# Merge stage of a hybrid decoder step: who says that a weight buffer is free, who copies the high parts, and how the sample sums reach the branch outputs

## The reference, cut to what matters

```
for each branch n:   m += sigmoid(x @ w_gate[n] + b_gate[n]) * (o_n @ w_branch[n])
x  = LN(ALPHA * x + m @ w_out);   x = LN(ALPHA * x + MoE(x))
```

## Time and profile before

| what | us |
|---|---|
| median of 3 runs (lowest, highest) | 1377.12 (1375.39, 1379.11) |
| the profiled execution's own time | 1373.24 |
| its span, first to last instruction | 1371.4 |
| TensorE busy (matmuls) | 1286.0, 94% of the span |
| VectorE busy | 944.2, 69% |
| ScalarE busy | 609.6, 44% |
| merge stage, 393.82 to 873.73 | 479.91 |

### The profile page before, as it was taken

How to read it: one execution, slowest core, us unless ns; L and a number is a source line. 1 busy time by engine, 2 the same in 40 slices (tenths; PEclk the granted TensorE clock), 3 DMA queues, 4 the chain that set the end, 5 groups by cost and what they waited for, 6 DMA issues and landing times.

```text
span 1371.4 us, 19929 instructions
## 1 busy us (share of the span) xinstructions
PE 1286.0 (94%) x7596; PEld 1087.6 (79%) x7596; DVE 944.2 (69%) x1492; ACT 609.6 (44%) x910; POOL 224.9 (16%) x199
## 2 busy tenths in 40 slices
PE   9999999998999999999999999999989999999970
PEld 5788657785589999999999999787748778888850
DVE  3674454433558878887877543466779799999957
ACT  4453565323642113121212112221338788898867
POOL 0200000007022322211010000000356212211130
PEclk9999999999999999999999999999989999999995
DMA  8223301002046776345553432322599986778986
GB/s 248 62 80 116 133 1 37 25 1 93 1 155 216 248 256 230 130 150 198 186 177 135 166 119 89 124 75 80 189 359 352 369 273 232 271 267 284 408 225 247
DMA packets 75011, 240.22 MB, mean 175 GB/s; under 512 B 16661, under 2 KB 27140, under 8 KB 61086
## 3 DMA queue, kind: packets, MB, share of 16 engines
q1 hardware_dynamic: 48630, 160.80, 32.5%
q0 software_dynamic: 17584, 61.31, 14.4%
q10 hardware_dynamic: 8704, 16.84, 3.4%
HBM read 215.65 MB, written 65.76 MB: 205 GB/s over the span
## 4 chain that ended last, share of the span: by engine, by line
PE 75%; DVE 6%; ACT 5%; DMA 4%; issue 2%; POOL 0%; SPq 0%; DVEq 0%; POOLq 0%; ACTq 0%
PE ps L568 18%; PE ps L570 17%; PE ps L569 17%; PE ps L1662 5%; PE ps L1693 3%; PE ps L1694 3%; PE ps L1695 3%; PE ps L1825 3%; PE ps L1865 2%; DMA b<-in_w 2%; DMA b<-in_w_merge 1%; ACT b L999 1%; ACT b L995 1%; ACT b L911 1%; PE ps L1857 1%
## 5 line engine op out<-in xcount | busy, mean ns | idle before, releaser
L568 PE MATMUL ps<-b,b 128*128 128x344 f32 (+2 forms) x1488 | 525.1, 353 | 9.0 <-DVE b L1016 5.0
L570 PE MATMUL ps<-b,b 128*128 128x344 f32 (+2 forms) x1488 | 516.3, 347 | 0.0
L569 PE MATMUL ps<-b,b 128*128 128x344 f32 (+2 forms) x1488 | 516.0, 347 | 0.0
L568 PEld LDWEIGHTS ps<-b,b 128*128 128x128 f32 (+1 forms) x1488 | 279.9, 188 | 33.6 <-DVE b L1016 5.6
L570 PEld LDWEIGHTS ps<-b,b 128*128 128x128 f32 (+1 forms) x1488 | 279.6, 188 | 24.5
L569 PEld LDWEIGHTS ps<-b,b 128*128 128x128 f32 (+1 forms) x1488 | 279.9, 188 | 21.1
L839 ACT ACTIVATE b<-ps,b 128x344 f32<-128x344 f32 x96 | 52.5, 548 | 276.6 <-PE ps L570 276.4
L1431 DVE TENSOR_TENSOR b<-b,b 128x2048 fp32r<-128x2048 f32 x64 | 146.5, 2291 | 19.4 <-ACT b L911 18.0
L1662 PE MATMUL ps<-b,b 128*128 128x128 f32 (+1 forms) x786 | 115.1, 278 | 14.3 <-DMA b<-tmp_xs 3.1
L911 ACT CAST b<-b 128x2048 fp32r<-128x2048 f32 x64 | 123.4, 1929 | 11.3 <-DMA b<-in_w 7.2
L1662 PEld LDWEIGHTS ps<-b,b 128*128 128x128 f32 (+1 forms) x786 | 91.1, 143 | 40.8 <-DMA b<-tmp_xs 5.2
(11 more groups left out here) (306 smaller groups left out, 1607.7 us busy)
## 6 DMA issues: line engine op xcount, KB each, us to landing
b<-in_w SPq DMA_DIRECT2D x96, 1024.0 KB
b<-in_w_merge SPq DMA_DIRECT2D x32, 640.5 KB, 4.0
tmp_xs<-b ACTq DMA_DIRECT2D x32, 514.0 KB, 4.1
b<-tmp_xs SPq DMA_DIRECT2D x32, 514.0 KB
b<-in_w_in SPq DMA_DIRECT2D x6, 1024.0 KB, 7.6
b<-in_xT SPq DMA_DIRECT2D x4, 1024.0 KB, 11.9
b<-in_w_out SPq DMA_DIRECT2D x4, 1024.0 KB, 8.5
b<-in_x SPq DMA_DIRECT2D x8, 512.0 KB, 4.1
```

Source lines behind the costliest of these rows:

```text
L568: mm(out, hi, mhi, start=start, stop=False)
L569: mm(out, hi, mlo, start=False, stop=False)
L570: return mm(out, lo, mhi, start=False, stop=stop)
```

## The change

Three edits are made together.

1. The loads of merge weights wait for the users of the buffer, not for `merge_free`. The first two are loaded as before. Weight j then waits for `mb` and `sgd` to have reached 3j-3: TensorE's last branch matmuls of unit 3j-4, and ScalarE's sigmoid of that unit (which reads the bias in the buffer). VectorE's increment of `merge_free` at each weight's end goes.
2. The six high parts of the branch outputs are copied by ScalarE, behind the sigmoid (and the weight copy) of units 4, 7, 35, 36, 41 and 44. VectorE's low parts move to units 8, 11, 38, 41, 45 and 48, and wait for the copy.
3. The partition sums of four samples are taken at once. `heads_out` goes. `partition_sums` has the ones as the stationary operand, 32 columns wide, and the sample's 256 values as the moving one; four samples go to four groups of 32 output partitions. It runs after units 37 and 41 for C and 57 and 72 for A. ScalarE copies the 512 columns of the bank out (at units 41 and 72), TensorE transposes them (four transposes, after units 42 and 73), and `decode_out` adds them at units 42 and 73 (before: 41 and 72), now by two adds. There are four pairs of accumulators instead of two, and VectorE waits for them in fewer places. SyncE's load of `w_out` waits for the transposes after unit 73 instead of for the sums after unit 72.

```diff
@@ emit_sp2
-                        w0 = sp.snap(i * 2 + (1 + u), min_val=1, max_val=4 * KD)
+                        used = sp.snap(i * 6 + (3 * u - 3), min_val=3, max_val=12 * KD)
-                        sp.wait_ge(S("merge_free"), w0)
+                        sp.wait_ge(S("mb"), used)
+                        sp.wait_ge(S("sgd"), used)
-            merge_weights(0, 26)
+            sp.wait_ge(S("merge_free"), 2)
+            for u in range(2):
+                sp.dma_start(wg[:, u, :], a["w_merge"][u]).then_inc(S(f"wg{u}"), 16)
+            merge_weights(2, 26)
             sp.wait_ge(S("mb"), 72)
-            sp.wait_ge(S("heads"), N("heads", 2 * NB))
+            sp.wait_ge(S("sums_T"), N("sums_T", 2))
@@ emit_pe2
+            def partition_sums(br, r):
+                pe.wait_ge(S("dv"), 4 * r + 4 if br else NB + 8 * r + 8)
...
+                for g in range(4):
+                    m = mm(ps[32 * g:32 * g + 32, 7, r * W:(r + 1) * W], one[:, 0:1].to_broadcast([P, 32]), acc_of(br, 4 * r + g),
+                           start=True, stop=True)
                 m.then_inc(S("heads"), 1)
+            def sums_transposed(br):
...
+                for k in range(4):
+                    m = tr(ps[:, 4, k * P:(k + 1) * P], nat_sums[br][:, k * P:(k + 1) * P])
+                m.then_inc(S("sums_T"), 1)
@@ emit_act2, decode
+                    if q == SUMMED[br][1]:
+                        act.wait_ge(S("heads"), N("heads", 2 * n))
+                        act.copy(nat_sums[br][:], ps[:, 7, :]).then_inc(S("sums_nat"), 1)
+                if q in HIGH_AT:
+                    n, f, tokens, keys = HIGH_AT[q]
...
+                    act.copy(oH[:, OUT_SLOT[n], f, 0:tokens], oT[:, n, f, 0:tokens]).then_inc(S("high"), 1)
@@ emit_dve2
-                    if b >= 2:
-                        dve.wait_ge(S("heads"), N("heads", NB + b - 1))
+                    if b == 0:
+                        dve.wait_ge(S("heads"), N("heads", 1))
+                    elif b == 2:
+                        dve.wait_ge(S("sums_T"), N("sums_T", 1))
...
+                if q in LOW_AT:
+                    n, f, tokens, count = LOW_AT[q]
+                    dve.wait_ge(S("high"), N("high", count))
+                    m = out_low(n, f, slice(0, tokens))
...
-                dve.sem_inc(S("merge_free"), 1)
@@ constants
+        HIGH_AT = {4: (3, 0, TOK, 0), 7: (3, 1, TOK, 0), 35: (2, 0, SEQ, 2 * NB - 1), 36: (2, 1, SEQ, 2 * NB - 1),
+                   41: (0, 0, SEQ, 2 * NB), 44: (0, 1, SEQ, 2 * NB)}
+        LOW_AT = {8: (3, 0, TOK, 1), 11: (3, 1, TOK, 2), 38: (2, 0, SEQ, 3), 41: (2, 1, SEQ, 4), 45: (0, 0, SEQ, 5), 48: (0, 1, SEQ, 6)}
+        SUMMED = {1: (VALUES_C + 5, VALUES_C + 9), 0: (VALUES_A + 17, VALUES_A + 32)}
```

More of the change, by code:

```diff
@@ L97, in build @@
             "pnew": ("lpre", 1), "onew": ("fb_mm", 1), "onT": ("faz", 1),
+            "sums_T": ("qk_tr_qkc", 8), "sums_nat": ("lsuf", 1), "high": ("qkT_qkc", 8),
         }
@@ L194, in build, with acc_of @@
         qA, qC = at(NAT, [P, 2, W]), at(NAT + 2048, [P, W])
-        acc_v = [at(NAT, [P, 2, W]), at(NAT + 2048, [P, 2, W])]
+        acc_v = [at(o, [P, 2, W]) for o in (NAT, NAT + 2048, TMP + 2944, TMP + 4992)]
+        nat_sums = [at(o, [P, 2 * W]) for o in (NAT, NAT + 2048)]
+        def acc_of(br, b):
+            return acc_v[((1, 0, 2, 1) if br else (0, 1, 2, 3))[b // 2]][:, b % 2, :]
         OB = TOKB // 4
@@ L604, in new_outputs @@
                 m.then_inc(S("onT"), 1)
[L606 to L611, removed]
-                m.then_inc(S("heads"), 1)
+            def partition_sums(br, r):
+                pe.wait_ge(S("dv"), 4 * r + 4 if br else NB + 8 * r + 8)
+                if br == 0 and r == 0:
+                    pe.wait_ge(S("sums_nat"), N("sums_nat", 1))
+                for g in range(4):
+                    m = mm(ps[32 * g:32 * g + 32, 7, r * W:(r + 1) * W], one[:, 0:1].to_broadcast([P, 32]), acc_of(br, 4 * r + g),
+                           start=True, stop=True)
+                m.then_inc(S("heads"), 1)
+            def sums_transposed(br):
+                pe.wait_ge(S("sums_nat"), N("sums_nat", 2 - br))
+                if br:
+                    pe.wait_ge(S("dp"), 2)
+                else:
+                    pe.wait_ge(S("os"), N("os", 4))
+                for k in range(4):
+                    m = tr(ps[:, 4, k * P:(k + 1) * P], nat_sums[br][:, k * P:(k + 1) * P])
+                m.then_inc(S("sums_T"), 1)
             def decode(q):
@@ L626, in decode @@
                         new_outputs(n)
[L627 to L630, removed]
+                for br, summed_at in SUMMED.items():
+                    if q in summed_at:
+                        partition_sums(br, summed_at.index(q))
+                    elif q == summed_at[1] + 1:
+                        sums_transposed(br)
             pe.wait_ge(S("x2"), N("x2", 2 * KD))
@@ L825, in decode @@
                         act.activation(s[:], s[:], ACT.Exp).then_inc(S("dex"), 1)
+                for n, br in ((1, 1), (2, 0)):
+                    if q == SUMMED[br][1]:
[3 more added lines that the diff above has]
+                    n, f, tokens, keys = HIGH_AT[q]
+                    if keys:
+                        act.wait_ge(S("ks"), keys)
+                    act.copy(oH[:, OUT_SLOT[n], f, 0:tokens], oT[:, n, f, 0:tokens]).then_inc(S("high"), 1)
             def weights_high(j):
@@ L1092, in value_sums @@
                 b, half = s // 2, s % 2
-                t, sums = value_tiles[value_slot(s)], acc_v[0][:, b % 2, :]
+                t, sums = value_tiles[value_slot(s)], acc_of(0, b)
                 link(dve.tensor_tensor(t[:, 0:4, :], t[:, 0:4, :], t[:, 4:8, :], ALU.add))
@@ L1111, in values_of_c @@
                 link(dve.tensor_tensor(v[:, 0, :], v[:, 0, :], v[:, 1, :], ALU.add))
-                if b >= 2:
-                    dve.wait_ge(S("heads"), N("heads", b - 1))
-                dve.tensor_tensor(acc_v[1][:, b % 2, :], v[:, 0, :], v[:, 2, :], ALU.add).then_inc(S("dv"), 1)
+                if b == 6:
+                    dve.wait_ge(S("heads"), N("heads", 1))
+                dve.tensor_tensor(acc_of(1, b), v[:, 0, :], v[:, 2, :], ALU.add).then_inc(S("dv"), 1)
             def new_values(n):
@@ L1125, in new_part, with decode_out @@
                                      ps[:, 6, 2 * NB * n:2 * NB * n + 2 * NB].rearrange("p (f b) -> p f b", f=2)))
-            def decode_out(br, count):
+            def decode_out(br):
                 new = slice(SEQ, TOK)
-                dve.wait_ge(S("heads"), N("heads", count))
-                link(dve.tensor_tensor(oT[:, 2 * br, :, new], oT[:, 2 * br, :, new],
-                                       ps[:, 7, 384 + 2 * NB * br:384 + 2 * NB * (br + 1)].rearrange("p (f b) -> p f b", f=2), ALU.add))
+                dve.wait_ge(S("sums_T"), N("sums_T", 2 - br))
+                for f in range(2):
+                    m = dve.tensor_tensor(oT[:, 2 * br, f, new].rearrange("p (r g) -> p r g", r=2),
+                                          oT[:, 2 * br, f, new].rearrange("p (r g) -> p r g", r=2),
+                                          ps[:, 4, :].rearrange("p (r f g x) -> p f r g x", r=2, f=2, g=4)[:, f, :, :, 0], ALU.add)
+                link(m)
                 link(dve.tensor_copy(oH[:, OUT_SLOT[2 * br], :, new], oT[:, 2 * br, :, new]))
                 out_low(2 * br, slice(0, 2), new).then_inc(S("os"), 1)
[L1135 to L1141, removed]
             def decode(q):
@@ L1157, in decode @@
                         new_part(n)
[L1158 to L1161, removed]
+                for br in range(2):
+                    if q == SUMMED[br][1] + 1:
+                        decode_out(br)
                 s, r = divmod(q - KEY_SLOT, 2)
@@ L1178, in decode @@
                         value_sums(s)
[L1179 to L1184, removed]
+                if q in LOW_AT:
+                    n, f, tokens, count = LOW_AT[q]
+                    dve.wait_ge(S("high"), N("high", count))
+                    m = out_low(n, f, slice(0, tokens))
+                    if f:
+                        m.then_inc(S("os"), 1)
+                    else:
+                        link(m)
             def merge_weight(j):
```

## The result

The changed kernel takes 1358.62 us (median of 4 runs, 1356.13 to 1359.26), against 1377.95 for the kernel before on the same chip (4 runs, 1375.39 to 1379.11): a ratio of 0.9859, 95% interval 0.9839 to 0.9878. That is 16.8 to 22.2 us less. The forecast was 1360.2, within 1355 to 1367.

A forecast was written before the change was run, and what follows sets the result against it. TensorE was taken to bound the merge stage. Removed 2.5 + 2.9 + 7.3 + 3.3 + 6.8 = 22.8 us, added 2.5 + 1.2 + 1.0 + 1.2 = 5.9, net 16.9: from 1377.12 to 1360.2 us, range 1355 to 1367.

The forecast's parts named there:

- What bounds, and what the most is: Merge stage: TensorE bounds; 479.9 us is 27.3 longer than bare matmuls, the most the change could give.
- Loads by their buffer's users: Weight loads, merge stage: issued at unit 3j-3's start, removing weight stalls of 2.5 and 2.9 us.
- The bound for a load that delays nobody: Weight loads, merge stage: one landing by 9.2 us after unit 3j-3's start delays no engine.
- Half clock: Units 43 to 51: pieces at 1.2 GHz following two stalls of 2.7 us and more go; 3.3 us booked.
- Partition sums: Sample sums in the merge stage: removes 6.8 us of small matmuls and 7.3 of waits; adds four at 0.63, 2.5.
- What is late next: Merge stage: two new TensorE stalls, 1.0 us after unit 35 and 1.2 at unit 51.
- The one behind unit 35: TensorE's transpose after unit 35 waits for VectorE's maximum of the A scores: new stall of 1.0 us.
- The one behind unit 50: At unit 51 TensorE waits for VectorE's weight: new stall of 0.9 us plus 0.3 for shared DMA queues, 1.2.
- More comes back: Rival: the two new stalls don't show (2.2 us less), sums at lower bound (1.1 less); 1357.5, chance 0.12.
- Doesn't do what it says: Rival: weights late by transfers, VectorE's lag its own; only 4 us come back, 1373, chance 0.04.
- VectorE takes the bound over: Rival: stalls of 3 to 5 us at unit 51 and after, low clock returns; gives back 7, 1367, chance 0.14.
- Slower: Rival: ScalarE's queue; the 30 loads land more than 11.3 us after unit 3j-3's start; 1382, chance 0.02.

The follow-up runs named there:

- e1_loads: The kernel before with the loads' edit alone (buffer's users instead of `merge_free`): 1365.22 us against 1376.38 for the kernel before, ratio 0.9912.
- e5_softmax35: The changed kernel with A's softmax one unit later (`SOFTMAX_A` 35 instead of 34): 1357.83 us, ratio 0.9858 to the kernel before.
- the repeated changed kernel: The changed kernel, nothing new in it, timed again beside two further versions on one chip: 1359.67 us, ratio 0.9889 to the kernel before.
- e8_load17_late: The changed kernel with weight 17's load held back until unit 48 is over: 1360.95 us in one execution alone, stage 466.89.
- e2_no_loads: The changed kernel with its loads waiting for `merge_free` again, other two edits kept: 1367.25 us against 1376.38 for the kernel before, ratio 0.9928.
- e4_low47: The changed kernel with the low part of unit 48 done in unit 47's work: 1357.26 us, ratio 0.9859 to the kernel before.
- e7_both: The changed kernel with value piece 4's gather put into piece 2's tile and A's softmax one unit later: 1355.49 us, ratio 0.9846 to the kernel before.

## Why the prediction was right, point by point

**What bounds, and what the most is.** Right. 27.3 us were booked as the whole that could come back, and 11.2 of them remain.

**Loads by their buffer's users.** Right in both terms, and in the reading that the wait behind unit 44 hung on the late copy: `e1_loads` brings 1.8 of it back without touching a sum. The issue comes 0.34 after the unit's start, as said, but for the two loads at 1.36. The price of a load was taken from the median of before, 4.0; it is 4.8 now (below). The bound for a load that delays nobody, 9.2, is too late: it leaves out the sigmoid of unit 3j-2, which stands behind the copy. Weight 11 landed 8.1 after its unit's start and VectorE was late by it.

**Half clock.** Booked at 3.3 and got back at 3.3: no piece in the changed kernel's stage. This was less safe than the text makes it. The prediction let "2.3 of idle didn't bring it, 2.7 did" stand as if there were a point between; `e5_softmax35` shows a piece behind 2.3, and the repeated changed kernel none behind 2.6.

**Partition sums.** Forecast 0.63 each, measured 0.77 three times and 0.56 once: 2.9 for four instead of 2.5. The column groups overlap, as in the earlier trace rows. With the prediction's 0.44 for the columns, 0.33 is left for the changes of mode, where it had 0.2; no run measures the two apart. The transposes were forecast at 0.6; the second set took 753.94 - 753.42 - 0.16 = 0.36 and 0.07 in the next matmul, so 0.43.

**What is late next.** Both places right. The one behind unit 35, forecast 1.0, cost 1.0 (the gap without its transpose), of which some 0.2 came from weight 11's load and not from the work that the prediction had counted. The one behind unit 50, forecast 1.2, cost 2.44: this is the mis-sized term. The step that failed is "It took part of the same transfers before [...], so I add only 0.3". Measured, the gathered piece is used 10.5 after unit 48's start instead of 8.9, 1.6 later, and `e8_load17_late` shows that it is the load. The Trainium skill's rule that was set against that number ("DMA: Bandwidth & Descriptors", Queues, rings and completion order: the engines take turns between queues by packets) gave up to 1.5 later and a stall of 2.4. The trace agrees with it in the stall and, against the kernel before, in the delay, and I had weighted it too low; against `e8_load17_late` the delay is 2.8, more than this estimate allows. Before the change the load was in flight only during the last half of the gather's way, and that was no measure of what it does from the start.

**The sum.** 16.9 was forecast and the stage gave 16.1: 1.2 too little was booked at unit 51 and 0.4 at the sums, 0.3 too much at the transposes, and the 0.5 that is left, found by difference alone, lies in what the removed parts gave back. That the total is within 0.8 is in part luck, since these errors cancel. The median of the runs fell by 19.3 at first and by 16.3 in the second set, so a hit of 1358.62 on 1360.2 is no finer than that spread.

**The rivals.** The time of "More comes back" doesn't follow from its terms: 2.2 and 1.1 less than 1360.2 are 1356.9, not 1357.5. "Doesn't do what it says" falls with `e1_loads` and `e2_no_loads`. "VectorE takes the bound over" is half there: one stall of 2.4, no low clock, and it vanishes when a gather moves. "Slower" needed loads that land after 11.3; the latest is copied from 8.9 after its unit's start on (weight 26, issued behind the w_out load).

## What to carry to other kernels

Free a buffer by those who read it, not by an engine that happens to finish later: the late load shows up as waits on engines that have nothing to do with it, here as a sum that TensorE waited for. When a transfer is moved forward, look at what it will share the DMA engines with from its first byte, and move first whichever of the two is needed soonest. Work taken off an engine brings nothing where that engine has slack, even if it is the one named in every wait: six copies changed the stage by less than 0.2 us, while one low part moved out of the chain by a unit (`e4_low47`) gave 1.5.

## What the runs showed that I had not expected

The idle time of TensorE doesn't decide alone whether half clock follows. In the merge stages of these kernels idle times of 2.3 (three profiles) and 2.6 were followed by full clock; of 2.3 (`e5_softmax35`), 2.4, 2.7, 2.8, 4.0 and 4.9 by a piece at 1.2 GHz. No row shown here tells the 2.3 with from the 2.3 without, so profiles of nearly equal kernels can differ by 1.7 us by that alone.

With the new issue time every second weight load starts together with ScalarE's two zero stores of 514 KB. The median from issue to landing went from 4.0 to 4.8, since from weight 3 to 13 and 17 to 31 the odd weights, which have the stores beside them, take 5.4 to 7.3, and most of the even ones 3.5 to 4.2:

```profile
b<-in_w_merge SPq DMA_DIRECT2D x32, 640.5 KB, 4.8
```

It costs little here: the up to 0.3 behind unit 35. In `e7_both`, where the softmax comes later, the median is 5.4 and TensorE waits for nobody in the stage.
